# Two attention blocks on one core: differential maps combined on GpSimd, one PSUM bank pair per unit

## What is computed

```python
def causal_block_attention(q, k, v, scale):
...
        s = jnp.einsum('bqhmd,bkhmd->bhmqk', q_blk, k).astype(jnp.float32) * scale
        s = jnp.where(mask, s, -jnp.inf)
        p = jax.nn.softmax(s, axis=-1).astype(v.dtype)
        return jnp.einsum('bhmqk,bkhd->bqhmd', p, v)
...
def diff_attention(q, k, v, q_gain, k_gain, lam_vecs, out_gain, cos, sin, layer_idx):
...
    o = causal_block_attention(q, k, v, DIFF_HEAD_DIM ** -0.5)
    lam = jnp.exp(jnp.sum(lv[0] * lv[1])) - jnp.exp(jnp.sum(lv[2] * lv[3])) + lam_init
    o = o[:, :, :, 0, :] - lam.astype(o.dtype) * o[:, :, :, 1, :]
    o = rmsnorm(o, out_gain) * (1.0 - lam_init)
```

## Time and profile before

| | |
|---|---|
| median of 3 runs | 3046.03 us (3041.13 to 3048.8) |
| profiled execution, its own time | 3044.45 us |
| its span in the trace | 3042.7 us |
| PE busy | 2788.1 us (92%) |
| GpSimd (POOL) busy | 1955.5 us (64%) |
| VectorE (DVE) busy | 1165.3 us (38%) |
| ScalarE (ACT) busy | 732.8 us (24%) |

### The profile page before, as it was taken

The page is one execution under the profiler, slowest core; times in us unless marked ns, Lnnn a source line. Parts: engine busy times, 40 slices in busy tenths (PEclk is TensorE's granted clock), DMA queues, the critical chain, the costliest instruction groups (busy, mean ns, idle before and its releaser), DMA issues. The chain is left out here.

```text
span 3042.7 us, 38827 instructions
## 1 busy us (share of the span) xinstructions
PE 2788.1 (92%) x14268; PEld 2256.7 (74%) x14268; DVE 1165.3 (38%) x1936; ACT 732.8 (24%) x1417; POOL 1955.5 (64%) x1562
## 2 busy tenths in 40 slices
PE   6988999999899997989899999899998999989997
PEld 5766777778788886667777778788887876777765
DVE  4278273311210113278173320310012387426773
ACT  3220454200130201221365210220111114212250
POOL 5767421788798895877420788788896772266704
PEclk9999999999999998999899999999998999989998
DMA  4312100233233333322100233223333321042202
GB/s 120 94 52 66 51 8 8 80 94 96 72 96 97 95 96 82 106 70 67 54 8 1 70 87 97 80 87 96 96 97 88 92 77 32 28 93 73 80 1 69
DMA packets 158902, 217.26 MB, mean 71 GB/s; under 512 B 51312, under 2 KB 62832, under 8 KB 158704
## 3 DMA queue, kind: packets, MB, share of 16 engines
q1 hardware_dynamic: 119952, 209.72, 23.6%
q10 hardware_dynamic: 38752, 4.95, 1.3%
HBM read 212.52 MB, written 2.10 MB: 71 GB/s over the span
## 5 line engine op out<-in xcount | busy, mean ns | idle before, releaser
L290 POOL TENSOR_TENSOR weight_parts<-weight_ring,zero 128x512 fp32r<-128x512 f32 x760 | 863.4, 1136 | 853.4 <-PE ps L375 453.0
L293 POOL TENSOR_TENSOR weight_parts<-weight_ring,weight_parts 128x512 fp32r<-128x512 f32 x780 | 1077.7, 1382 | 62.8 <-ACT weight_parts L301 2.6
L377 PE MATMUL ps<-h_feature_major_high,weight_parts 128*128 128x512 f32 x2304 | 584.6, 393 | 19.5 <-DVE h_feature_major_low L471 6.6
L377 PEld LDWEIGHTS ps<-h_feature_major_high,weight_parts 128*128 128x128 f32 x2304 | 430.4, 189 | 124.8 <-POOL weight_parts L290 11.2
L375 PE MATMUL ps<-weight_parts,h_feature_major_high 128*128 128x512 f32 (+1 forms) x1920 | 463.0, 381 | 34.5 <-DVE h_feature_major_low L1613 9.1
L375 PEld LDWEIGHTS ps<-weight_parts,h_feature_major_high 128*128 128x128 f32 x1920 | 341.8, 194 | 119.0 <-issue 21.9
L377 PE MATMUL ps<-h_feature_major_low,weight_parts 128*128 128x512 f32 x1152 | 309.4, 390 | 0.0
L375 PE MATMUL ps<-weight_parts,ut_high 128*128 128x512 f32 x1024 | 254.6, 390 | 0.0
L377 PEld LDWEIGHTS ps<-h_feature_major_low,weight_parts 128*128 128x128 f32 x1152 | 216.9, 188 | 45.8
L375 PE MATMUL ps<-weight_parts,h_feature_major_low 128*128 128x512 f32 (+1 forms) x960 | 239.1, 376 | 0.0
L507 PE MATMUL ps<-arena 64*128 64x512 f32 (+9 forms) x704 | 172.9, 488 | 56.0 <-ACT probs L563 23.1
(11 more groups left out here) (231 smaller groups left out, 2930.7 us busy)
## 6 DMA issues: line engine op xcount, KB each, us to landing
weight_ring<-in_w_in SPq DMA_DIRECT2D x344, 256.0 KB, 2.7
weight_ring<-in_w_mlp SPq DMA_DIRECT2D x256, 256.0 KB, 2.7
weight_ring<-in_w_out SPq DMA_DIRECT2D x64, 256.0 KB, 2.6
weight_ring<-in_w_mem_kv SPq DMA_DIRECT2D x32, 256.0 KB, 2.9
weight_ring<-in_w_diff_o SPq DMA_DIRECT2D x32, 256.0 KB, 2.6
weight_ring<-in_w_mla_o SPq DMA_DIRECT2D x16, 256.0 KB, 2.6
weight_ring<-in_w_cross_o SPq DMA_DIRECT2D x16, 256.0 KB, 2.6
arena<-in_mem SPq DMA_DIRECT2D x2, 1024.0 KB, 5.2
```

Source lines behind the costliest of these rows:

```text
L290: self.nc.gpsimd.tensor_tensor(high, raw, self.m["zero"][:].broadcast_to([P, raw.shape[1]]), ALU.add).then_inc(self.s["slab_high"], 1)
L293: self.nc.gpsimd.tensor_tensor(low, raw, high.bitcast(F32), ALU.subtract).then_inc(self.s["slab_split"], 1)
L377: last = self.nc.tensor.matmul(banks[:, t, :], w[:, cut], h, **ends)
```

## The change

1. **Maps joined early.** For a differential unit VectorE works out 1/sum and the ratio -lambda * sum1 / sum2 right after exp (`ratio`, one round behind maximum). GpSimd multiplies the second map by the ratio and adds it to the first, in SBUF. Then only one map is turned, copied and weighted, and finish is one instruction. GpSimd also scales latent q and k, now one piece behind each of the last eight joins.
2. **One bank pair per unit.** Unit u owns banks 2(u mod 4) and the next: its scores, then its transposes, then its result. scores(u) waits for finish(u-4). PE's round is turn(i-3), scores(i), weight(i-3); ScalarE copies with a lag of 3. The probabilities get a third buffer. This holds for all four attention stages.
3. **Tail.** Where a projection follows a stage, the last two rounds lie before its chunks 1 and 3 (before: 1 and 2), and the first projection after a stage waits for finish instead of exp.
4. **Equal halves.** Three pairs of projections are cut into equal widths: 512 + 256 becomes 336 + 336, 340 + 340 and 326 + 326.

```diff
-        parts = [(0, A.scores), (2, A.turn), (3, A.weight)]
+        parts = [(3, A.turn), (0, A.scores), (3, A.weight)]
...
-            self.first_wait[name] = (self.s["finished" if self.order.index(name) % 2 else "exped"], hi)
+            self.first_wait[name] = (self.s["finished"], hi if self.order.index(name) % 2 else hi - 2)
...
-            self.project(pe, *projection, {1 + k: f for k, f in enumerate(tail)})
+            self.project(pe, *projection, {1 + 2 * k: f for k, f in enumerate(tail)})
...
+    def pair(self, u):
+
+        return self.m["ps"][:, 2 * (u % 4):2 * (u % 4) + 2, :]
+
+    def joins(self, u):
+
+        return self.units[u]["kind"] == "diff"
+
+    def maps(self, u):
+
+        return 1 if self.joins(u) else 2
+
+    def result(self, u):
+
+        return self.pair(u)[:, 1 if self.joins(u) else 0, 0:2 * P]
+
+    def probs(self, u):
+
+        return self.slots(u)
+
     def scores(self, u):
         pe, a = self.nc.tensor, self.units[u]
-        if u >= 2:
-            pe.wait_ge(self.s["exped"], u - 1)
+        if u >= 4:
+            pe.wait_ge(self.s["finished"], u - 3)
...
     def turn(self, u):
         pe, a = self.nc.tensor, self.units[u]
-        pe.wait_ge(self.s["exped"], u + 1)
-        if u >= 1:
-            pe.wait_ge(self.s["turned_copied"], u)
-        for j in range(2):
+        if self.joins(u):
+            pe.wait_ge(self.s["joined"], sum(map(self.joins, range(u + 1))))
+        else:
+            pe.wait_ge(self.s["exped"], u + 1)
+        for j in range(self.maps(u)):
             for kb in range(0, a["n"], P):
-                src = self.m["probs"][:, u % 2, j, kb:min(kb + P, a["n"])]
+                src = self.probs(u)[:, j, kb:min(kb + P, a["n"])]
                 width = src.shape[1]
-                dst = self.m["ps"][0:width, 4 + j, kb:kb + P]
+                dst = self.pair(u)[0:width, j, kb:kb + P]
...
     def weight(self, u):
         pe, a = self.nc.tensor, self.units[u]
         pe.wait_ge(self.s["turned_copied"], u + 1)
-        if u >= 2:
-            pe.wait_ge(self.s["finished"], u - 1)
         blocks, rows = max(1, a["n"] // P), min(P, a["n"])
-        for j in range(2):
+        for j in range(self.maps(u)):
             for kb in range(blocks):
-                last = pe.matmul(self.m["ps"][:, 6 + u % 2, j * P:(j + 1) * P],
+                last = pe.matmul(self.result(u)[:, j * P:(j + 1) * P],
...
-        last = dve.tensor_reduce(out, self.m["ps"][:, 2 * (u % 2):2 * (u % 2) + 2, 0:a["n"]],
-                                 AX.X, ALU.max, negate=True)
+        last = dve.tensor_reduce(out, self.pair(u)[:, :, 0:a["n"]], AX.X, ALU.max, negate=True)
...
-        if u >= 2:
-            act.wait_ge(self.s["turned"], u - 1)
+        if u >= 3:
+            act.wait_ge(self.s["turned"], u - 2)
...
-        act.activation(self.m["probs_t"][0:rows, u % 2, :, 0:width], self.m["ps"][0:rows, 4:6, 0:width],
+        rows, width, maps = min(P, a["n"]), max(P, a["n"]), self.maps(u)
...
-        "lat0": tok(w_in, C_LAT, W512), "lat1": tok(w_in, C_LAT + W512, 256),
+        "lat0": tok(w_in, C_LAT, LATW // 2), "lat1": tok(w_in, C_LAT + LATW // 2, LATW // 2),
...
+    third = [view(outs, 4096, 2, W512), view(arena, 16384, 2, W512)]
+    A = Attention(nc, m, s, units, lambda u: m["probs"][:, u % 3] if u % 3 < 2 else third[u >= U2])
...
-            def scale_mla():
-
-                pool.wait_ge(s["mla_scales"], 1)
-                for src, st in ((qm, st_qm), (km, st_km)):
-                    for t in range(TT):
-                        nc.gpsimd.tensor_tensor(src[:, t], src[:, t], bc(st[:, t, :], [P, MH, MQK], 2),
-                                                ALU.mult).then_inc(s["mla_roped"], 1)
-
-            L.split_slabs(pool, {"gate00": scale_mla})
+            def join_maps_and_scale_mla():
+
+                scaled = [(src[:, t], st[:, t, :]) for src, st in ((qm, st_qm), (km, st_km)) for t in range(TT)]
+                for u in range(U1, U2):
+                    n, r = units[u]["n"], m["recip"][:, u % 8, :]
+                    first, second = (A.probs(u)[:, j, 0:n] for j in range(2))
+                    pool.wait_ge(s["ratios"], u - U1 + 1)
+                    nc.gpsimd.tensor_scalar(second, second, r[:, 1:2], None, ALU.mult).then_inc(s["scaled"], 1)
+                    pool.wait_ge(s["scaled"], u - U1 + 1)
+                    nc.gpsimd.tensor_tensor(first, first, second, ALU.add).then_inc(s["joined"], 1)
+                    k = u - (U2 - len(scaled))
+                    if k >= 0:
+                        if k == 0:
+                            pool.wait_ge(s["mla_scales"], 1)
+                        src, st = scaled[k]
+                        nc.gpsimd.tensor_tensor(src, src, bc(st, [P, MH, MQK], 2), ALU.mult).then_inc(s["mla_roped"], 1)
+
+            L.split_slabs(pool, {"gate00": join_maps_and_scale_mla})
...
-            A.steps(U1, U2, (2, A.copy), (0, A.exp), between={prep_rounds[-2]: lambda: roots(st_both)})
+            A.steps(U1, U2, (3, A.copy), (0, A.exp), between={prep_rounds[-2]: lambda: roots(st_both)})
...
+            act.wait_ge(s["weighted"], U2)
+            A.steps(U2, U3, (3, A.copy), (0, A.exp))
...
+            def ratio(u):
+                r, total = m["recip"][:, u % 8, :], m["rowsum"][:, u % 8, :]
+                dve.wait_ge(s["exped"], u + 1)
+                v.reciprocal(r, total)
+                v.drain()
+                v.tensor_scalar(r[:, 1:2], r[:, 1:2], total[:, 0:1], lam_neg, ALU.mult, ALU.mult).then_inc(s["ratios"], 1)
+
             def finish(u):
                 a = units[u]
                 dve.wait_ge(s["weighted"], u + 1)
                 r = m["recip"][:, u % 8, :]
-                v.reciprocal(r, m["rowsum"][:, u % 8, :])
-                v.drain()
-                sums = ps[:, 6 + u % 2, 0:2 * P]
+                sums = A.result(u)
                 i, p2 = a["i"], a["pair"]
                 if a["kind"] == "diff":
-                    dst = od[:, i, p2 * P:(p2 + 1) * P]
-                    v.tensor_scalar(dst, sums[:, P:2 * P], r[:, 1:2], lam_neg, ALU.mult, ALU.mult)
-                    v.drain()
-                    v.scalar_tensor_tensor(dst, sums[:, 0:P], r[:, 0:1], dst, ALU.mult, ALU.add).then_inc(s["finished"], 1)
+                    v.tensor_scalar(od[:, i, p2 * P:(p2 + 1) * P], sums[:, 0:P], r[:, 0:1], None, ALU.mult).then_inc(s["finished"], 1)
                     return
+                v.reciprocal(r, m["rowsum"][:, u % 8, :])
+                v.drain()
...
-            A.steps(U1, U2, (0, A.maximum), (3, finish), between=dict(zip(prep_rounds, pieces)))
+            A.steps(U1, U2, (0, A.maximum), (1, ratio), (3, finish), between=dict(zip(prep_rounds, pieces)))
...
-        "za0": tok(w_in, 0, W512), "za1": tok(w_in, W512, 256),
-        "zb0": tok(w_in, Z_B, W512), "zb1": tok(w_in, Z_B + W512, 256),
+        "za0": tok(w_in, 0, A_W // 2), "za1": tok(w_in, A_W // 2, A_W // 2),
+        "zb0": tok(w_in, Z_B, B_W // 2), "zb1": tok(w_in, Z_B + B_W // 2, B_W // 2),
```

41 lines of the change are left out of this document (19 added, 22 removed).

## The result

The changed kernel takes 3171.22 us (median of 4 runs, 3168.72 to 3173.89) against 3045.7 us, a ratio of 1.041 with an interval of 1.040 to 1.043. It is slower by about 125 us. The forecast was 3134 with a range of 3085 to 3185.

What follows compares the result with a forecast made beforehand. PE, busy 92% of the span, was taken as the bound before, a serial PE-VectorE loop after. Per layer 3 + 9 + 10 + 17 + 5 + 6 - 6 = +44, two layers +88: 3134 us, range 3085 to 3185.

Steps and rivals of the forecast that it cites:

- The mechanism: All attention stages: scores wait for finish four units back, making one serial loop through PE and VectorE each round.
- Cross stage: Same loop, 2.57 us per unit against 2.19 for eight units: +3 with the wait before the first latent projection.
- Differential stage: Loop of 10.45 us per head plus pieces, GpSimd scalings, fill and drain: 107.5 against 98.5 us, +9 per layer.
- the whole lock: Differential stage: GpSimd's joins and VectorE's large pieces delay each other through the shared port, +5 per layer, bounds 0 and 10.
- Latent stage: Group of four takes 14.45 us against 11.84: +9.5, plus +0.5 for the gate projection waiting for finish.
- Second block: Its units lose the hidden wait for scores; with dsa units, fill and drain: +17 us.
- The tail: After the latent stage, the gate projection's first half waits for finish: +0.5.
- Equal halves: Three projection pairs: PE saves 12 in all, cut for GpSimd's thin margin to -6 per layer, bounds -2 and -12.
- The loop has slack: Rival, chance 0.10: finish returns in time, the loop binds nothing, PE's savings show, 2987 us.
- about the same: Rival, chance 0.03: differential gain cancels losses of latent, cross and second block, 3036 to 3053 us.
- A second limit on top: Rival, chance 0.14: lock holds whole joins, or differential-stage clock stays at 1.2 GHz; 3160 to 3200 us.
- GpSimd as the bound: Rival, chance 0.03: joins cost 1.6 times the splits, differential stage follows GpSimd, about +15 per layer, 3165 us.

Runs made afterwards that it cites:

- e4: Changed kernel's join and halves with the old kernel's banks and tail, turn and weight one lag later in the differential stage: 3034.34 us, ratio 0.998.
- e7: e4 with GpSimd's joins cut to the first key column, other columns left out: 2992.18 us, ratio 0.983.
- e3: Changed kernel with both GpSimd instructions of a join cut to the first key column, other columns left out: 3149.01 us, ratio 1.036.
- e8: Changed kernel with finish before maximum everywhere, weight before scores and copy lag 2 outside the differential stage, old tail: 3115.1 us, ratio 1.022.
- e5: Changed kernel with VectorE's finish put ahead of maximum in all four attention stages: 3337.75 us, ratio 1.097.
- e1: Kernel before the change with only the equal halves added: 3013.49 us, ratio 0.992.
- e6: Changed kernel with a stage's last two turns right behind its last round and the weights ahead of chunks 1 and 2: 3142.11 us, ratio 1.033.
- e12: Old banks, equal halves, third probabilities buffer; only the last 11 differential units joined, on VectorE, the others as before the change: 3010.57 us, ratio 0.990.
- e11: Kernel before the change with the equal halves and a third buffer for probabilities: 3019.52 us, ratio 0.992.
- e10: e4 with GpSimd joining only the first 21 differential units and VectorE the other 11: 3012.34 us, ratio 0.991.

## Why the prediction held, and where it was off

**The mechanism** was right: scores wait for finish through one serial loop in all four stages, shown by the waits, by e4 (old banks, lags and tail: -137 us), by e7 beside e3 (22 to 25 us per differential stage) and by e8 (same banks, other order: the cross and latent stages as before). One part of it was incomplete. I priced the loop on PE and VectorE; e5 shows that ScalarE's order, copy behind the exp of an earlier round, is a link too. In the latent stage the first full group took 15.4 us instead of 14.45, and 0.67 of that lie in the one round (507.72 to 511.69, forecast 3.3) in which weight waits for such a copy.

One sign that I had named as right did not come: PE's busy sum was to fall by over 100 us, and it stayed (2789.0 against 2788.1). My own terms for it add up to 77 (3.3 us for each of 16 heads and 12 per layer for the equal halves), and I had left out that the same matmuls are busy for longer at a lower clock, 0.94 in the mean of the run against 0.96. I also named a differential stage near 107 us as a sign, where my sum, with lock and clock, has 118.5; it took 118.7.

**The sum.** Forecast +88, measured +124 between the traces. Term by term, both layers, against e1:

| term | forecast | measured |
|---|---|---|
| cross, differential, latent stages | 2 x 33 | +70.7 |
| second block's units | 2 x 17 | +47.0 |
| tails behind cross and latent stages | in the above, under 3 | +21.5 |
| clock in the latent transposes | none | +3.9 |
| equal halves (e1 to before) | -12 | -31.5 |
| everything between | none | +12.7 |

- *Cross stage*, +3 with the wait ahead of the first latent projection: 4.3 and 4.2 in the stage alone. A unit took 2.77 us, forecast 2.57.
- *Differential stage*, +9, +5 for the shared port and +6 for the clock: 20 forecast, 20.3 and 21.6 measured. Scalings by GpSimd are 5.4 us longer than alone, against 5 forecast for the whole lock; e3's 7.4 and 12.1 for all of GpSimd's work stand against 4 + 5. The clock was 0.83 in the stage instead of 0.98; what it alone costs was not measured apart. A join was priced too low: the joins of a head take 8.5 us (rows of lines 793 and 795: 68.2 us for eight heads), not 6.7.
- The rule of the Trainium skill, "SBUF — State Buffer", section "Who interferes with whom", that instructions of VectorE and GpSimd can lock each other out, agrees in direction. In the differential stage the delay is mostly GpSimd's (0.79 against 0.60 us at 128 columns, while the pieces grew from 949 to 986 ns). Behind the latent stage of the changed kernel it falls on both: VectorE's operation of 1024 columns takes 1.23 us beside an idle GpSimd and 1.87 beside its splits, and the second half of GpSimd's slab split (line 293) takes 2.16 us there and 1.26 where it starts while VectorE runs nothing of that kind. In these rows the one that starts second is the one that takes longer.

```profile
568.64 1.23 DVE L1206 TENSOR_TENSOR probs<-outs 128x1024 f32<-128x1024 f32 x1
...
577.42 1.87 DVE L1206 TENSOR_TENSOR probs<-outs 128x1024 f32<-128x1024 f32 x1
```

```profile
577.17 1.03 POOL L290 TENSOR_TENSOR weight_parts<-weight_ring,zero 128x512 fp32r<-128x512 f32 x1
578.28 2.16 POOL L293 TENSOR_TENSOR weight_parts<-weight_ring,weight_parts 128x512 fp32r<-128x512 f32 x1
...
581.51 1.26 POOL L293 TENSOR_TENSOR weight_parts<-weight_ring,weight_parts 128x512 fp32r<-128x512 f32 x1
```

- *Latent stage*, +9.5 and +0.5: 9.8 and 10.5 measured. That this agrees is luck: full groups grew by 3.6 and 3.9 us, not 2.6, and the last stretch by 6.0, while the first shrank by 3.7, for the most part because the stage started at full clock.
- *Second block*, +17: 22.1 and 25.1. Mis-sized: I kept the old clock there. A stretch of it now runs at 0.79 against 0.92; how much of the 5 to 8 us is clock was not tried apart.
- *The tail* is the term that was missed. I let "the gate projection's first half now waits for finish, +0.5" stand for the whole of it. The blocks of turn, copy wait and weight ahead of chunks 1 and 3, the slow clock on the first chunks and the later start of VectorE's norms cost 7.4 and 5.3 us behind the latent stage, and 4.5 and 4.4 behind the cross stage, 21.5 in all; in the same four stretches e6 gets 22.4 us back.
- *Equal halves*, -6 per layer of both blocks: 31.5 in all, 15.5 to 16 per layer (e1), outside the bounds of 2 to 12. The sum of PE's own times, 12, was right for the stretches with these projections (11.6 per layer); the cut for GpSimd's thin margin was not. The gain that was set too low and the tail and second block that were set too low cancel in part, which is luck: without the 19.5 us that the halves gave beyond the forecast, the measured time would lie above the range.
- The remaining 12.7 us are spread over projections far from the change. e12, whose code there is that of before, also has +5.7 us in the 580 us between the first layer's merge and the second layer's cross stage. That part is not explained by the change, and stays open.

**The rivals.** "The loop has slack" is out by the waits, and "about the same" by the result. "A second limit on top" was partly true: PE waits 18.6 us for joins in the first differential stage, though 7.4 us is all that the stage gains when they are nearly free (e3). "GpSimd as the bound" holds for the end of the stage, where the scalings stand between the joins: it is busy 20.5 of the 21 us from 452 to 473, and the last head takes 23.0 us to the transposes against 19.9 with joins of one column (e3).

## What to carry to other kernels

When a buffer's reuse is moved to the last step of a pipeline, write out the round of each in-order engine and follow the new wait through all of them: four buffers in flight were worth nothing here, since the release stood behind work of the next round, and in the cross and latent stages the same buffers with weight ahead of scores ran like the old ones. Work taken off the busiest engine pays only if what carries it instead has room at that very time: the join was worth 12 us per layer when it cost nothing, and lost 8 on GpSimd. And price the end of a stage as carefully as its steady round.

## What the runs showed of the hardware

- On GpSimd, multiplying 128 x 512 values by a per-partition scalar took 1.56 us alone, and adding two such tiles 1.26: one input less was not faster.
- In the last 7 us of the changed kernel's differential stage PE was busy 4.61 us, at a granted clock of 0.50. The 128 transposes behind it, without any gap, took 16.44 us instead of 14.14: the clock was 0.50 from 473.1 to 477.5 us, then 1.00 from 479 us on, while PE did nothing but transposes. Before, it was 1.00 throughout:

```profile
473.10 16.44 PE L391 MATMUL ps<-ident,arena 128*96 128x128 f32 x128
```

- The clock also fell behind a stretch without a gap. After 14 us of such transposes at 1.00 and a pause of 1.9 us, the next four scores of 512 columns took 3.69 us in e1 (0.51 from 460.8 to 464.2 us), 2.83 in e11, and 1.98, at full clock, in e10, e12 and the changed kernel. How busy the stage ahead had kept PE does not sort these runs: the latent stage ran at 0.90 in e1 (PE busy 88.1 of 98.5 us in the differential stage) and in e7 (67.0 of 86.2), and at 0.97 in e12 (80.1 of 95.9) and e10 (73.3 of 97.2); in e4 it was 0.97 in one layer and 0.90 in the other. What decides it stays open. It is worth 2.3 us a time: all by which e10's latent stage is shorter than e1's lies in its first group (11.7 against 14.0).
- VectorE and GpSimd delay each other, and which of them loses differs by stretch: 1.87 against 1.23 us on VectorE and 2.16 against 1.26 on GpSimd behind the latent stage, 1.09 against 0.92 on GpSimd at 256 columns in the differential one.
